# A 31-tap depthwise convolution split into even and odd samples, three half-length filters in sixteen 32x32 tiles of TensorE

## The chip, the core and the metric

One Trainium2 (trn2) chip, one core. The time is the device time in microseconds from launch to end of one execution. The kernel is one program for a whole network block of two parts. Times of several executions agree closely, so a median of three is given.

## What is computed

The reference runs a first transformer block (attention in three branches, a linear recurrence, a feed-forward part) and then a second one with two layers. The change is in the second block. Cut to what matters, one layer of it is:

```python
h = h + 0.5 * swiglu_ffn(rms_norm(h), w_gate_up, w_down)        # ffn "a"
q, k, v, ca, cg = split(rms_norm(h) @ w_in)
attn = sliding_window_attention(rope(q), rope(k), v, sinks)     # 8 heads of 64
u = ca * sigmoid(cg)                                            # 256 tokens x 512 channels
y = depthwise_conv(u, conv_w, taps=31, causal) + conv_b
conv = silu(layer_norm(y, ln_g, ln_b))
h = h + concat(rms_norm(attn), rms_norm(conv)) @ w_out
h = h + 0.5 * swiglu_ffn(rms_norm(h), ...)                      # ffn "b"
e = rms_norm(p @ w_ple)                                         # 256 -> 1024, the "embedding"
h = h + sigmoid(h @ w_ple_gate) * e
```

All data are float32. There are 256 tokens, 1024 features, 512 channels in the convolution, and two such layers. Each channel has its own 31 taps, and y at token s is the sum over j of w[j] * u[s - 30 + j].

## The kernel before, in words

The kernel is written engine by engine: SyncE (SP) loads weights, ScalarE (ACT), VectorE (DVE), GpSimd (POOL) and TensorE (PE) each run a list of instructions in a fixed order, and semaphores tie them together. Each engine works its list strictly in order, so the order written there is the schedule. The two layers are unrolled; only the wide chunks of the feed-forward parts run in hardware loops.

**Weights and products.** A matrix product is a "chunk": 512 output columns for 256 tokens. Its weights come in units of two k-tiles (256 x 512; one k-tile for w_ple) through a ring of 8 stage buffers. ACT copies a unit to w_hi in the reduced format fp32r (`split`, L760), DVE subtracts to get w_lo (`split`, L1417), and PE multiplies hi by hi, hi by lo and lo by hi (L2375 to L2377), each product of 512 columns being one instruction. There are 4 hi/lo slots, so ACT can split a unit only when PE has used the unit four before it. Chunks write alternately to the two PSUM buffers `acc[0]` and `acc[1]`. `CHUNKS` counts them, and a chunk waits until the buffer's last user has been read (`acc_free`). PSUM has two more pairs of banks: `turns` (two banks `turn[0]`, `turn[1]`, used in rotation for transposes and small results, counted by `TURNS`, released by `turn_free`) and `pair` (two banks for scores and the convolution; `score` is its first, counted by `SCORES`). That is all of PSUM. A float32 product that isn't split (transposes L2388, scores L2413, the convolution L2863, means L2930, L2942, L2959) is two instructions on PE, each with its own weight load.

**The order of a layer on PE** around the change (L2856 to L2964): chunks Lq, Lkv, Lcg and Lca with the attention's small products between them, then

- `Lple0`, the first half of p @ w_ple (two k-tiles of 6 products), and ahead of its second k-tile the transposes of the first half of u (`conv_in_turn(0)`, L2913);
- the transposes of the second half of u (L2919), then `Lple1`, the second half of p @ w_ple (12 products);
- the convolution (`conv`, L2867), which waits for `s_in_place` (u_t written), `s_diag` and `s_mixo`;
- a wait for `s_mixlo` (x_lo of the attention half), then `Lout_a0` with the row means of the squared attention output ahead of its first k-tile (L2942) and the first mean over the features ahead of its third (`feature_means(0)`, L2926); `Lout_a1` with the second mean ahead of its first k-tile; `Lout_c0` with the row means of the convolution's half ahead of its last k-tile (L2959); `Lout_c1`.

**The convolution before.** The 512 channels lie on partitions in quads of 32. A tap is a diagonal 32x32 matrix. Two neighbouring taps share one product: partitions 0 to 31 of a pair of quads hold u and partitions 32 to 63 hold u shifted by one token, and the weights are two diagonals on top of each other (64 rows, 32 columns). `diag` holds them for 14 pairs of taps, written by DVE during the chunk `La_dn0` (`diagonals`, L2099 to L2110, eight instructions). PE uses eight tiles of 64x32 at once: 4 groups of channels by 2 row groups, each product with 256 columns (all tokens). There are two halves, each of 14 pairs of taps:

```python
for half in range(2):
    wait(pe, s_in_place, Count(half + 1, [(layer, 2)]))
    for j in range(PAIRS_PE):
        mm = conv_round(half, ..., j == 0, j == PAIRS_PE - 1)
```

To bring the shifted copies in place, ACT and DVE each write eight 32x256 pieces per half from the transposes' bank to `u_t` (`shifted_pairs` L587, L1293, L2160). The last three taps are left to DVE, straight from that bank with per-partition weights and the bias (`late_taps`, L2165 to L2182, into y_late), and `y = pair + y_late` (L2200) follows the convolution. The taps themselves reach `taps2` earlier, in chunk d0 of the first block: POOL loads them in two DMAs to `rawt` (L725), PE transposes them, and DVE moves them with 33 small copies (L1994, L1997).

**The layer norm.** DVE adds y by pairs of channel groups into two `group_sums` (`sum_groups`, L2205); PE multiplies each by a matrix of 1/512 into `score`, adding the two (L2930); DVE centres y (L2220); ACT squares it (L1311), DVE sums again (L2205), PE makes the second mean, ACT takes the root (L1321), DVE the reciprocal (L2231) and the scaling (L2234). ACT then applies silu and writes x_hi (L1328, L1334), DVE x_lo (L2238), for the four k-tiles of `Lout_c0` and `Lout_c1`. A third sum of squares gives the row means (L2959).

**ACT's order** in this stretch (L1284 to L1350): split Lple1; split Lout_a0 unit 0; the shifted copies of half 0; split Lout_a0 unit 1; the copies of half 1; the square of the attention output `att_sq` (L1296), whose halves POOL adds (L740, L743); x_hi of the attention half (L1300); both halves of e_ple out of PSUM (`embedding_out`, L1224); split Lout_a1; the squares of e_ple's first half (L1230); a table load and the root of the row means (L1316); the layer norm's part.

**DVE's order** (L2141 to L2262): u (L2147), split Lple1, a copy of the attention's last result (L1577), for each half the shifted copies and the late taps, split Lout_a0, x_lo of the attention half (L2193), split Lout_a1 unit 0, y, the sums, split Lout_a1 unit 1, the reciprocal of the row means' root, the centring, the sums of squares, the residual of Lout_a0 (L1489), and so on.

## Time and profile before

| | |
|---|---|
| median of 3 runs | 1395.59 us (1395.32 to 1395.7) |
| the profiled execution | 1395.72 us, its span 1393.9 us |
| PE busy | 1382.3 us, 99% of the span, 8063 instructions and as many weight loads |
| DVE busy, ACT busy | 973.1 us (70%), 827.2 us (59%) |
| granted TensorE clock | 0.999 of full speed on average |
| DMA | 249.62 MB, mean 179 GB/s |

The profile is one execution. The span runs from the first to the last instruction on the core; the execution's own time is 1.8 us more. Busy PE time counts pipelined instructions to their modelled ends, so neighbours overlap: what an instruction costs PE is the distance from its start to the next start, not its duration. PEld are weight loads, which run beside the products.

### The profile page before, as it was taken

To read this page: it belongs to the slowest core of one execution; us is meant where nothing else is said; L and a number is where in the kernel's file an instruction comes from. 1 tells how busy PE (TensorE), PEld (TensorE's weight loads), DVE (VectorE), ACT (ScalarE), POOL (GpSimd) and SP (SyncE) were. 2 spreads that over 40 slices of the span, in tenths; PEclk is the share of its full clock that TensorE was granted. 3 is DMA by queue.
4 is the path that set the end of the run, shared out by engine and by line. 5 is a ranking of instruction groups with operands and counts; after the bars stand their busy time and mean duration, and the time that the engine had idled before them with its cause. 6 is when DMAs were issued, how large, how long until landed. Compare 5 with 4: busy or idle time off the path is not lost.

```text
span 1393.9 us, 21622 instructions
## 1 busy us (share of the span) xinstructions
PE 1382.3 (99%) x8063; PEld 1163.7 (83%) x8063; DVE 973.1 (70%) x1408; ACT 827.2 (59%) x1267; POOL 21.4 (2%) x33
## 2 busy tenths in 40 slices
PE   9999999999999999999999999999999999999997
PEld 7777788888888888887888888888888878888886
DVE  5878866775657777568876675676775779777755
ACT  7689755554356554478765554565544687655544
POOL 2100000000000000000000000000000000000000
PEclk9999999999999999999999999999999999999999
DMA  9933555566566666443566665566655435666650
GB/s 289 342 95 107 166 194 175 193 194 197 191 183 202 186 188 203 152 152 114 153 197 193 191 213 185 167 188 190 194 197 156 149 106 152 205 187 189 214 186 31
DMA packets 130157, 249.62 MB, mean 179 GB/s; under 512 B 8552, under 2 KB 12992, under 8 KB 130080
## 3 DMA queue, kind: packets, MB, share of 16 engines
q1 hardware_dynamic: 127680, 240.58, 54.8%
q0 software_dynamic: 2240, 7.73, 1.8%
q8 instruction: 50, 0.82, 0.2%
q10 hardware_dynamic: 160, 0.27, 0.1%
q14 instruction: 27, 0.22, 0.0%
HBM read 247.49 MB, written 1.05 MB: 178 GB/s over the span
## 4 chain that ended last, share of the span: by engine, by line
PE 99%; DVE 0%; ACT 0%; issue 0%; POOL 0%; DVEq 0%; ACTq 0%; POOLq 0%
PE acc L2375 16%; PE acc L2377 16%; PE acc L2376 16%; PE acc L2741 14%; PE pair L2741 7%; PE acc L2747 7%; PE turns L2741 6%; PE pair L2747 4%; PE turns L2747 3%; PE turns L2388 3%; PE pair L2863 2%; PE pair L2413 1%; PE turns L2434 1%; PE acc L2460 1%; PE turns L2529 0%; PE pair L2510 0%
## 5 line engine op out<-in xcount | busy, mean ns | idle before, releaser
L1417 DVE TENSOR_TENSOR w_lo<-stage,w_hi 128x1024 fp32r<-128x1024 f32 (+2 forms) x462 | 549.8, 1200 | 293.5 <-ACT w_hi L760 288.1
L760 ACT ACTIVATE w_hi<-stage 128x1024 fp32r<-128x1024 f32 (+2 forms) x462 | 475.6, 1039 | 405.4 <-PE acc L2377 195.5
L2741 PE MATMUL acc<-x,w_hi 128*128 128x512 f32 x832 | 229.1, 393 | 0.0
L2741 PEld LDWEIGHTS acc<-x,w_hi 128*128 128x128 f32 x832 | 149.3, 189 | 26.1 <-DVE x L1471 0.8
L2375 PE MATMUL acc<-w_hi,x_hi 128*128 128x512 f32 (+2 forms) x432 | 170.5, 395 | 0.1
L2377 PE MATMUL acc<-w_hi,x_lo 128*128 128x512 f32 (+2 forms) x432 | 163.8, 379 | 0.0
L2376 PE MATMUL acc<-w_lo,x_hi 128*128 128x512 f32 (+2 forms) x432 | 163.8, 379 | 0.0
L2375 PE MATMUL acc<-w_hi,g_hi 128*128 128x512 f32 x352 | 137.4, 390 | 0.0
L2376 PE MATMUL acc<-w_lo,g_hi 128*128 128x512 f32 x352 | 137.0, 389 | 0.0
L2377 PE MATMUL acc<-w_hi,g_lo 128*128 128x512 f32 x352 | 137.0, 389 | 0.0
L2747 PE MATMUL acc<-x,w_lo 128*128 128x256 f32 x832 | 136.2, 282 | 0.0
L2747 PEld LDWEIGHTS acc<-x,w_lo 128*128 128x128 f32 x832 | 122.5, 190 | 8.1
L2741 PE MATMUL pair<-x,w_hi 128*128 128x512 f32 x448 | 123.4, 390 | 0.0
L2741 PE MATMUL turns<-x,w_hi 128*128 128x512 f32 x384 | 102.8, 390 | 0.0
L2741 PEld LDWEIGHTS pair<-x,w_hi 128*128 128x128 f32 x448 | 84.1, 188 | 18.2
L2375 PEld LDWEIGHTS acc<-w_hi,x_hi 128*128 128x128 f32 x432 | 81.3, 188 | 20.9 <-issue 6.5
L2377 PEld LDWEIGHTS acc<-w_hi,x_lo 128*128 128x128 f32 x432 | 81.2, 188 | 15.9
L2376 PEld LDWEIGHTS acc<-w_lo,x_hi 128*128 128x128 f32 x432 | 81.4, 188 | 13.3
L2741 PEld LDWEIGHTS turns<-x,w_hi 128*128 128x128 f32 x384 | 72.1, 188 | 15.5
L2377 PEld LDWEIGHTS acc<-w_hi,g_lo 128*128 128x128 f32 x352 | 66.1, 188 | 13.7
L2375 PEld LDWEIGHTS acc<-w_hi,g_hi 128*128 128x128 f32 x352 | 66.1, 188 | 13.5
L2376 PEld LDWEIGHTS acc<-w_lo,g_hi 128*128 128x128 f32 x352 | 66.1, 188 | 13.4
(388 smaller groups left out, 1778.3 us busy)
## 6 DMA issues: line engine op xcount, KB each, us to landing
stage<-in_ffn_w_gate_up SPq DMA_DIRECT2D x176, 512.0 KB, 3.7
stage<-in_ffn_w_down SPq DMA_DIRECT2D x88, 512.0 KB, 4.4
stage<-in_w_ff SPq DMA_DIRECT2D x64, 512.0 KB, 4.1
stage<-in_w_in SPq DMA_DIRECT2D x62, 512.0 KB, 4.4
stage<-in_w_out SPq DMA_DIRECT2D x16, 512.0 KB, 3.8
stage<-in_w_ple_gate SPq DMA_DIRECT2D x16, 512.0 KB, 4.3
stage<-in_w_lru_up SPq DMA_DIRECT2D x8, 512.0 KB, 3.7
stage<-in_w_o SPq DMA_DIRECT2D x8, 512.0 KB, 4.4
```

The source lines that it names most:

```text
L760: act.activation(w_hi[:, n.slot(SPLIT), 0:t, 0:w], stage[:, n.slot(STAGE), 0:t, 0:w], ACT.Copy).then_inc(hi_done, 1)
L1417: dve.tensor_tensor(w_lo[:, n.slot(SPLIT), 0:t, 0:w], stage[:, n.slot(STAGE), 0:t, 0:w], w_hi[:, n.slot(SPLIT), 0:t, 0:w].bitcast(F32), AL ...
L2375: pe.matmul(dst, xh, wh, start=kt == 0, stop=False)
L2376: pe.matmul(dst, xh, wl, start=False, stop=False)
L2377: mm = pe.matmul(dst, xl, wh, start=False, stop=kt == last)
L2388: mm = pe.transpose(turn[n.slot(2)][0:cols_in, at:at + rows_in], src, ident[0:rows_in, 0:rows_in])
L2413: mm = pe.matmul(pair[:, i, k * w:(k + 1) * w], q[half, 2 * g + a, t * P:(t + 1) * P], keys[half, kbase + g, 0:w], start=k == 0, stop=k == ...
L2434: mm = pe.matmul(turn[n.slot(2)][i * HD:(i + 1) * HD, at:at + 2 * P], v(0 if m == 0 else x, g), src, start=m == 0 or x == 0, stop=m == 0 o ...
L2460: return pe.matmul(acc[c][:, t, :], rows[:, i * UNIT_K + q, t * P:(t + 1) * P], weights[:, n.slot(SPLIT), q, :], start=start, stop=stop)
L2741: pe.matmul(banks[m], w_hi[:, n.slot(SPLIT), q, m * P:(m + 1) * P], x2[:, kt, :], start=kt == 0, stop=False)
L2747: mm = pe.matmul(banks[m][:, S:], w_lo[:, n.slot(SPLIT), q, m * P:(m + 1) * P], x2[:, kt, 0:S], start=False, stop=kt == KD - 1)
L2863: mm = pe.matmul(pair[c * QUAD:(c + 1) * QUAD, k, half * S:(half + 1) * S], weights(rows_in, n), src(rows_in, n), start=first, stop=last)
```

## The change

The convolution is computed on even and odd samples ("phases"). With e and o the even and odd samples of u, and with the 32 taps (the 32nd is zero) also split in two interleaved sets of 16, each phase of the output needs two 16-tap filters of 128 samples, four in all. Three do: one filter on the odd samples with the difference of the sets, one on the even samples with another difference, and one on the sum e + o, whose result enters both phases. `taps2` now holds the three sets, `u_t` the two phases, `u_sum` their sum.

- Each filter is 16 taps x 16 tiles of 32 rows by 32 columns with 128 columns moving. The first and the third filter write to `pair` and `turns` (one bank for each row group), the sum's filter to both `acc` buffers, for which `CHUNKS` has two more entries and `TURNS` two more (`Lconv`).
- All 31 taps are done by PE; the late taps and the shifted copies are gone. ACT copies one bank of transposed u to `u_t` and DVE the other, each in one instruction; DVE writes `u_sum` in one. ACT moves the sum's result with the bias to `conv_sum` in four instructions, and y is `pair` or `turns` plus `conv_sum`.
- DVE writes twelve groups of 16 diagonals (512 elements) in place of eight of 14 (448). The first four wait for the last g_lo of the feed-forward part, since they lie in its buffers.
- u is written in two instructions with its blocks of 32 channels permuted.
- Both transposes of u stand ahead of the second k-tile of `Lple0`. `Lple1` stands behind the convolution, and so does, on ACT, the second half of e_ple, between the two splits of `Lout_a1`.
- Each mean over the features is one product of `all_sums`, for which DVE adds the two `group_sums` first; the row means likewise. `feature_means(0)` stands ahead of the first k-tile of `Lout_a0`, not the third, and the wait for `s_mixlo` there too.
- The taps are loaded by eight small DMAs behind a memset and moved by five DVE instructions.

```diff
-TAP_PAIRS = (TAPS2 + 1) // 2
-PAIRS_PE = 14
-LATE = TAPS2 - 2 * PAIRS_PE
+PHASES = 2
+TAPS_P = (TAPS2 + 1) // PHASES
+S_P = S // PHASES
+FILTERS = 3
...
+        def conv_bank(r):
+            return (pair, turns)[r // 2][:, r % 2, :]
+        def sum_bank(r, layer):
+            return acc[CHUNKS.at(f"Lu_sum{r // 2}", 0, layer).slot(2)][:, r % 2, 0:S_P]
+        def in_phases(half):
+            return u_t[:, :, 2 * half:2 * half + 2, TAPS_P - 1:].rearrange("p h a n -> p a h n")
+        def of_tokens(x):
+            return x.rearrange("p (a n h) -> p a h n", a=2, h=PHASES)
...
@@ ACT
                 split("Lple1", layer)
+                act.wait_ge(s_zero, 3)
+                n = TURNS.at("Lu", 0, layer)
+                wait(act, turn_done, n + 1)
+                act.activation(in_phases(0), of_tokens(turn[n.slot(2)][:, :]), ACT.Copy).then_inc(turn_free[n.slot(2)], 1)
                 split("Lout_a0", layer, units=[0])
-                act.wait_ge(s_zero, 3)
-                for k in range(2):
-                    if k == 1:
-                        split("Lout_a0", layer, units=[1])
-                    n = TURNS.at("Lu", k, layer)
-                    wait(act, turn_done, n + 1)
-                    for copy_to, copy_from in shifted_pairs(k, range(KC // 2), turn[n.slot(2)]):
-                        ins = act.activation(copy_to, copy_from, ACT.Copy)
-                    ins.then_inc(s_shifted, 1)
+                embedding_out(0)
                 wait(act, s_mixo, Count(2, [(layer, 1)]))
...
-                for c in range(2):
-                    embedding_out(c)
-                split("Lout_a1", layer)
+                split("Lout_a0", layer, units=[1])
                 embedding_squares(0)
+                wait(act, s_conv_sum, Count(1, [(layer, 1)]))
+                for r in range(KC):
+                    at = V2["conv_b"] + r
+                    ins = act.activation(conv_sum[:, r, :], sum_bank(r, layer), ACT.Identity,
+                                         bias=vec2[:, layer, at:at + 1])
+                    if r % 2:
+                        ins.then_inc(acc_free[CHUNKS.at(f"Lu_sum{r // 2}", 0, layer).slot(2)], 1)
+                split("Lout_a1", layer, units=[0])
+                embedding_out(1)
+                split("Lout_a1", layer, units=[1])
...
@@ DVE
-                for half in range(2):
-                    shifted_half(half)
-                    late_taps(half)
+                n = TURNS.at("Lu", 1, layer)
+                wait(dve, turn_done, n + 1)
+                dve.tensor_copy(in_phases(1), of_tokens(turn[n.slot(2)][:, :])).then_inc(turn_free[n.slot(2)], 1)
+                turns_read(dve, "Lu", 2, layer)
+                dve.tensor_tensor(u_sum, u_t[:, 0, :, :], u_t[:, 1, :, :], ALU.add).then_inc(s_u_sum, 1)
                 split("Lout_a0", layer)
...
-                split("Lout_a1", layer, units=range(1))
-                wait(dve, s_conv, Count(1, [(layer, 1)]))
+                wait(dve, turn_done, TURNS.at("Lconv", 1, layer) + 1)
                 for k in range(2):
+                    evacuated(dve, f"Lu_sum{k}", layer)
                     of = slice(2 * k, 2 * k + 2)
...
                 wait(dve, s_yin, Count(2, [(layer, 2)]))
-                for half in range(2):
-                    sum_groups(y, half)
-                split("Lout_a1", layer, units=range(1, 2))
+                for k in range(2):
+                    dve.sem_inc(turn_free[k], 1)
+                summed = note(dve.tensor_tensor(group_sums[:, :, :], y[:, 0:2, :], y[:, 2:4, :], ALU.add))
+                sum_halves(summed)
+                split("Lout_a1", layer)
...
                 for half in range(2):
                     wait(dve, s_ysq, Count(half + 1, [(layer, 4)]))
-                    sum_groups(ysq, half)
+                    summed = sum_groups(ysq, half)
+                sum_halves(summed)
...
@@ PE
+                def conv_taps(src, weights, bank):
+                    for q in range(TAPS_P):
+                        for n in range(KC):
+                            for r in range(KC):
+                                rows_in = slice(r * QUAD, (r + 1) * QUAD)
+                                mm = pe.matmul(bank(r)[n * QUAD:(n + 1) * QUAD, :], weights[rows_in, n, q, :],
+                                               src[rows_in, n, q:q + S_P], start=q == 0, stop=q == TAPS_P - 1)
                     return mm
                 def conv():
-                    for half in range(2):
-                        wait(pe, s_in_place, Count(half + 1, [(layer, 2)]))
...
+                    turns_read(pe, "Lu", 2, layer)
+                    conv_taps(u_t[:, 1, :, :], diag[:, :, 1, :, :], lambda r: conv_bank(r)[:, 0:S_P])
+                    wait(pe, s_u_sum, Count(1, [(layer, 1)]))
+                    for k in range(2):
+                        c = CHUNKS.at(f"Lu_sum{k}", 0, layer)
+                        wait(pe, acc_free[c.slot(2)], c.lap(2))
+                    conv_taps(u_sum, diag_sum, lambda r: sum_bank(r, layer)).then_inc(s_conv_sum, 1)
+                    conv_taps(u_t[:, 0, :, :], diag[:, :, 0, :, :],
+                              lambda r: conv_bank(r)[:, S_P:S]).then_inc(turn_done, 2)
...
-                chunk("Lple0", pl_hi, pl_lo, layer, ready=lambda kt: conv_in_turn(0) if kt == 1 else None)
-                conv_in_turn(1)
-                chunk("Lple1", pl_hi, pl_lo, layer)
-                wait(pe, s_mixo, Count(2, [(layer, 1)]))
+                chunk("Lple0", pl_hi, pl_lo, layer, ready=conv_in_turns)
                 wait(pe, s_diag, Count(1, [(layer, 1)]))
                 free(SCORES, score_free, "Lsum", 0, layer)
                 conv()
+                chunk("Lple1", pl_hi, pl_lo, layer)
...
                     free(SCORES, score_free, "Lsum", i, layer)
-                    for half in range(2):
-                        wait(pe, s_group_sum, Count(2 * i + half + 1, [(layer, 6)]))
-                        mm = pe.matmul(score[:, 0:S], mean, group_sums[:, half, :], start=half == 0, stop=half == 1)
-                    mm.then_inc(score_done, 1)
+                    wait(pe, s_group_sum, Count(i + 1, [(layer, 3)]))
+                    pe.matmul(score[:, 0:S], mean, all_sums, start=True, stop=True).then_inc(score_done, 1)
                 pe.wait_ge(s_zero, 3)
-                wait(pe, s_mixlo, Count(2, [(layer, 2)]))
```

## Rows read from the trace of the kernel before

**Rows 1.** The page: busy us (share) xinstructions, granted clock in 40 slices, instruction queue.
```profile
PE 1382.3 (99%) x8063; PEld 1163.7 (83%) x8063; DVE 973.1 (70%) x1408; ACT 827.2 (59%) x1267; POOL 21.4 (2%) x33
...
PEclk9999999999999999999999999999999999999999
...
q8 instruction: 50, 0.82, 0.2%
```

**Rows 2.** The page: the chain that ended last, by engine.
```profile
PE 99%; DVE 0%; ACT 0%; issue 0%; POOL 0%; DVEq 0%; ACTq 0%; POOLq 0%
```

**Rows 3.** Timeline of PE, first layer: start us, us, engine, line, operation, count.
```profile
648.73 0.39 PE L2377 MATMUL acc<-w_hi,pl_lo 128*128 128x512 f32 x1
649.05 13.17 PE L2863 MATMUL pair<-u_t,diag 64*32 64x256 f32 x448
662.15 0.61 PE L2942 MATMUL turns<-masks,xs 128*128 128x1 f32 x4
```

**Rows 4.** The same, second layer.
```profile
1139.26 12.32 PE L2863 MATMUL pair<-u_t,diag 64*32 64x256 f32 x448
1152.21 0.58 PE L2942 MATMUL turns<-masks,xs 128*128 128x1 f32 x4 [0.63 <-issue]
```

**Rows 5.** Timeline of DVE, second layer.
```profile
1150.44 1.67 DVE L2193 SCALAR_TENSOR_TENSOR x_lo<-mixt,vec,x_hi 128x256 fp32r<-128x256 f32 x4
...
1153.16 1.28 DVE L2200 TENSOR_TENSOR y<-pair,pt 128x512 f32<-128x512 f32 x2
```

**Rows 6.** Timeline of PEld over 0.09 us: one round's weight loads.
```profile
649.29 0.15 PEld L2863 LDWEIGHTS pair<-u_t,diag 64*32 64x32 f32 x8
```

**Rows 7.** Groups of PEld in the first layer's convolution: count, busy us, mean ns.
```profile
L2863 PEld LDWEIGHTS pair<-u_t,diag 64*32 64x32 f32 x448 | 9.4, 105 | 3.7 <-issue 1.2
```

**Rows 8.** Timeline of PE: 16 fp32 instructions of 128 columns in two tiles.
```profile
613.30 1.16 PE L2413 MATMUL pair<-kt,qt 64*128 64x128 f32 x16
```

**Rows 9.** Timeline of PE: the two means over the features, then the row means.
```profile
665.44 1.02 PE L2930 MATMUL pair<-sig,masks 128*128 128x256 f32 x4
666.12 0.58 PE L2375 MATMUL acc<-w_hi,x_hi 128*128 128x512 f32 x1
...
669.07 1.02 PE L2930 MATMUL pair<-sig,masks 128*128 128x256 f32 x4
...
679.83 0.95 PE L2959 MATMUL pair<-masks,sig 128*128 128x1 f32 x8
```

**Rows 10.** Timeline of PE ahead of the convolution, first layer.
```profile
643.94 0.60 PE L2388 MATMUL turns<-ct,sm 128*128 128x128 f32 x4
645.53 0.39 PE L2377 MATMUL acc<-w_hi,pl_lo 128*128 128x512 f32 x1
```

**Rows 11.** Timeline of DVE ahead of the convolution, first layer.
```profile
643.94 0.42 DVE L1577 COPY mixt<-turns 128x256 f32<-128x256 f32 x1
```

**Rows 12.** Groups of DVE from 532 to 562 us: count, busy, mean ns, idle before.
```profile
L1417 DVE TENSOR_TENSOR w_lo<-stage,w_hi 128x1024 fp32r<-128x1024 f32 x12 | 14.6, 1222 | 7.8 <-ACT w_hi L760 7.6
L2105 DVE TENSOR_TENSOR diag<-vec,taps 128x448 f32<-128x448 f32 x8 | 4.4, 617 | 0.0
```

**Rows 13.** Timeline of ACT around the layer norm, first layer.
```profile
652.42 1.06 ACT L1296 ACTIVATE xs<-mixt 128x1024 f32<-128x1024 f32 x1
653.38 1.69 ACT L1300 ACTIVATE x_hi<-mixt,vec 128x256 fp32r<-128x256 f32 x4
655.10 1.94 ACT L1224 ACTIVATE e_ple<-acc 128x1024 f32<-128x1024 f32 x2
...
660.16 1.28 ACT L1316 ACT_TABLE_LOAD   x1
```

**Rows 14.** Timeline of DVE around the layer norm, first layer.
```profile
666.51 1.29 DVE L2220 SCALAR_TENSOR_TENSOR y<-pair,y 128x512 f32<-128x512 f32 x2 [0.28 <-PE pair L2930]
667.94 0.98 DVE L2205 TENSOR_TENSOR sig<-sm 128x256 f32<-128x256 f32 x2
669.36 1.41 DVE L1489 SCALAR_TENSOR_TENSOR h<-acc,stat,h 128x512 f32<-128x512 f32 x2 [0.43 <-PE acc L2377]
```

More of the change, by code:

```diff
@@ L723, in _ @@
             wait(pool, s_rstd, RSTD.at("norm2", 1))
+            pool.memset(rawt, 0.0).then_inc(s_raw_rows, 1)
+            pool.wait_ge(s_raw_rows, 1)
             for l in range(LAYERS):
-                pool.dma_start(rawt[:, l, :], a["conv_w_2"][l].rearrange("j (r p) -> (j r) p", p=P)).then_inc(s_raw, 16)
+                by_tile = a["conv_w_2"][l].rearrange("j (r a m) -> a j r m", a=KC, m=QUAD)
+                for tile in range(KC):
+                    pool.dma_start(rawt[tile * QUAD:tile * QUAD + TAPS2, l, :].rearrange("j (r m) -> j r m", m=QUAD),
+                                   by_tile[tile]).then_inc(s_raw, 16)
             wait(pool, s_h, RESIDUAL.at("d", 3))
@@ L1229, in embedding_squares @@
                 for t in range(TT):
-                    act.activation(hid2[:, t, :, :].rearrange("p t n -> p (t n)"), e_ple[:, t, c * COLS:(c + 1) * COLS],
+                    if c or t:
+                        wait(act, s_ple, Count(2 * c + t, [(layer, 4)]))
+                    act.activation(pt2[:, 1, 0:COLS], e_ple[:, t, c * COLS:(c + 1) * COLS],
                                    ACT.Square, scale=1.0 / D ** 0.5,
@@ L2954, in row_means @@
                     if kt == 3:
-                        wait(pe, s_group_sum, Count(6, [(layer, 6)]))
+                        wait(pe, s_group_sum, Count(3, [(layer, 3)]))
                         free(SCORES, score_free, "Lsum", 2, layer)
                         for t in range(TT):
-                            for half in range(2):
-                                mm = pe.matmul(score[:, t:t + 1], group_sums[:, half, t * P:(t + 1) * P], mean[:, 0:1],
-                                               start=half == 0, stop=half == 1)
+                            mm = pe.matmul(score[:, t:t + 1], all_sums[:, t * P:(t + 1) * P], mean[:, 0:1],
+                                           start=True, stop=True)
                         mm.then_inc(score_done, 1)
```

147 lines of the change are left out of this document (63 added, 84 removed).

## The prediction

> **What bounds the kernel now.** I read the page first: TensorE is busy 99% of the span, at the full granted clock in all 40 slices [rows 1], and the chain that ended last is 99% PE [rows 2]. So a microsecond counts only if PE itself gets or loses it, by its own instructions or by a wait; DVE (70%) and ACT (59%) matter where PE stands waiting for them. Next comes the timeline of PE around the convolution. In the first layer 448 fp32 instructions of 256 columns run from 649.05 us until the row means start at 662.15: 13.10 us [rows 3]. In the second they run from 1139.26 to 1152.21, 12.95 us, of which 0.63 us is a gap before the row means [rows 4]; DVE's timeline names it: the last x_lo of the attention half ends at 1150.44 + 1.67 = 1152.11 [rows 5]. One instruction lasts 0.375 us to its end, so 448 in 12.32 us are 56 rounds of eight tiles with a period of (12.32 - 0.375) / 55 = 0.217 us [rows 4]. That is the time in which 256 columns pass twice. The eight weight loads of a round leave within 0.15 us, the last of them lasting 0.105, so they are (0.15 - 0.105) / 7 = 6.4 ns apart [rows 6, 7]. Within a round PE issues for 45 ns and then streams.
>
> **The convolution.** The three filters have 16 taps each over 128 columns, in sixteen tiles: 3 x 16 = 48 products per tile, each two instructions, so 96 rounds of sixteen (1536 instructions and as many loads). No row shows sixteen tiles. The nearest rows give a period from two sides. Half of 0.217 is 0.109 us, and sixteen starts 6.4 ns apart need 0.103: they just fit. The score products, fp32 of 128 columns in two tiles, take (1.16 - 0.285) / 7 = 0.125 us a round where the last lasts about 0.285, but with weights of 128 columns [rows 8]. I take 0.112, near the lower end, because its tiles have the same 32-column weights, and keep 0.107 and 0.125. That gives 96 x 0.112 = 10.75 us and 0.2 for the drain behind it, 10.95 in place of 13.10 and 12.95: **-2.15 and -2.0 us** (with 0.125: -0.9 and -0.75). The second layer's gap is counted here: it goes because the second embedding product now stands between the convolution and the row means.
>
> On the supply of instructions the trace proves only the rate of now, 896 records in 12.3 us or 13.7 ns each; asked for are 3072 in 10.75, or 3.5 ns each. The 50 packets of the instruction queue take 0.2% of 16 engines' span, 0.2% x 16 x 1394 / 50 = 0.9 us apiece, and hold 16.4 KB [rows 1]. The Trainium skill ("Runtime: NRT & Kernel Launch", Instruction fetch mechanics) says that such a block is 256 instructions and that PE's memory holds 2048 of them. By it 3072 records are twelve blocks, 10.8 us if they come one behind the other with nothing ahead, and eight of them are there already. The trace agrees with the block: 50 packets can't carry 16,126 records unless the bodies of the loops stay resident.
>
> A rule of the skill speaks against the change: "TensorE: Matmul & The Clock Gate", Wait — 56ns, not 53.3ns, gives about 25 ns as the least distance of two matmul starts. By that rule the convolution would take 1536 x 0.025 = 38 us. The loads of rows 6 are 6.4 ns apart, but for eight only; sustained, rows 4 have 26.7 ns a product, so the trace doesn't exclude it.
>
> **The means.** Each mean over the features is two fp32 products of 256 columns (four instructions, (1.02 - 0.378) / 3 = 0.214 us apart by their own group [rows 9]) and becomes one: 2 x 0.214 saved, twice a layer, 0.86. The row means go from eight instructions to four, at (0.95 - 0.24) / 7 = 0.10: 0.41 saved [rows 9]. **-1.27 us a layer**, all on PE's queue.
>
> **Ahead of the convolution.** Both turns of u now stand behind the first k-tile of the first embedding product; the 2.9 us of the second no longer cover the copies. The first turn starts at 643.94 [rows 10]; the second needs the bank that DVE's copy leaves at 644.36 [rows 11], so it runs about 644.4 to 645.1 with its latency. Then ACT and DVE each copy one bank of 512 elements, 0.64 us by half of the 1.28 of two such reads [rows 5]: in place at 645.8. PE meanwhile has six products, up to about 646.3 (in rows 10 the same six end 0.23 us behind 645.53, 1.8 us after the turn started). **No wait**, slack 0.5 us. DVE gives up 32 shifted copies and the late taps (both engines had 3.1 to 3.5 us per half) for one copy and one sum of 572 elements. u, now two instructions with permuted blocks, costs DVE perhaps 0.1 more and has 1 us of cover.
>
> **Diagonals.** Eight instructions of 448 elements (4.4 us) become twelve of 512, 4.4 x 12/8 x 512/448 = 7.5 us. DVE idles 7.8 us in that stretch [rows 12]; 3.1 more fits. Zero; with no cover it would be up to 3.1 us a layer. The taps' 33 small copies become five; POOL issues eight small DMAs instead of two and a memset, over 100 us before they are read. Zero.
>
> **ACT in the convolution.** Behind its copy: a split (1.06), one half of e_ple (1.94 / 2), the square (1.06), x_hi (1.69) [rows 13], a split, the squares of the embedding (about 1.7), the four moves of the sums (about 1.3): 8.8 us, within 10.95. The first half of e_ple frees the bank of the second filter, which PE wants 3.6 us after the start; ACT is there after some 2.2.
>
> **Behind the convolution.** Let E be its end. PE: twelve products, 2.95 us by the distance of 666.12 and 669.07 [rows 9], then the row means 0.5, so mean 0 is wanted at E + 3.5. DVE: y 1.28, one sum of 512 elements 0.65, one of 256 0.42, with gaps 2.6: in time. Mean 1 is wanted at E + 3.5 + 0.43 + 5.7 = 9.6. ACT is what is **late next**: the second half of e_ple can start only at E + 2.95 (0.97), then a split 1.06, the table load 1.28 [rows 13], the root 0.26: E + 6.5. DVE waits for that before it centres (1.29), while ACT splits and then squares twice 0.62: E + 9.1; the last sums, now with one more step of 0.42 behind two of 0.38 [rows 14], end at about E + 10.0. **+0.4 us of wait a layer** (between 0 and 1.5). The chain from mean 1 to the first product of the convolution's half of w_out starts with the residual (1.41) [rows 14] as before and stays. The row means of the convolution's half had about 1.1 us of slack and lose 0.4.
>
> **The sum.** -2.15 - 2.0 - 2 x 1.27 + 2 x 0.4 = -5.9 us. The profiled execution took 1395.72 (span 1393.9 with 1.8 around it), so 1389.8; the median of the runs, 1395.59, is 0.13 below it: **1389.7**. A measurement of this kernel can tell about 0.2%, 2.8 us.
>
> **Rivals.**
> (1) Sixteen tiles don't run at once: the array or the four row groups that add into the same partitions let eight through, and a round takes 0.217 us. Then the convolution takes 96 x 0.217 + 0.2 = 21.0 us, +7.9 and +8.1; with the means the time is about 1409: slower. For it: no row has more than eight. Against it: the change gives each row group its own bank, and the starts are 6.4 ns apart. It decides from a period of (13.0 + 1.27 - 0.4) / 96 = 0.144 us. Instructions fetched late would cost the same way, but as gaps: the 50 packets served at most 16,126 / 50 = 322 records each [rows 1], so 3072 take ten or more; at 0.9 us they just fit, at twice that, one by one, they are 18 us and the time is near 1403. Together 0.15.
> (2) The issue floor of the skill's page binds. As a mechanism here it is one product each 25 ns, just under the 26.7 of rows 4: 25.4 us more a layer, near 1444. 0.04.
> (3) The convolution runs as forecast or near 0.125, but ACT's late second half costs PE 1 to 2 us a layer or the slack ahead of the convolution is negative: 1392 to 1394. For it: five things stand on ACT's queue before the root. 0.18.
> My forecast, -4.8 to -7.7 us, has 0.61; 0.02 is left for what I don't see.
>
> **Numbers.** Faster by over 2.8 us: the forecast and half of (3), 0.70. Within: the rest of (3) and a little of (1), 0.12. Slower: 0.18. The range goes down to 1387 (a period of 0.107, no waits: -7.7, and a little) and up to 1396, which takes in all of (3); what is left out is (1) and (2). The likeliest case's own range is 1387.5 to 1391.
>
> **What would show it.** In the changed timeline 1536 instructions in 10.6 to 10.9 us from first start to last end; no gap before them; the first instruction of the second embedding product 0.2 to 0.3 us behind the last start; means of two instructions; a gap of 0.2 to 0.6 before mean 1 with DVE's last sum as its releaser. A convolution over 13.9 us, or gaps in it, would prove me wrong on the sign; a wait over 1 us at the first filter, at mean 0 or at mean 1 would be rival 3.

## The result, and the profile after

The changed kernel takes 1459.24 us (median of six runs, 1455.67 to 1462.26) beside 1395.64 us for the kernel before (1395.32 to 1395.96): a ratio of 1.0455, 95% interval [1.0444, 1.0466], **slower by 63.6 us**. I had forecast 1389.7. The profiled execution took 1459.78 us with a span of 1458.0.

Page of the changed kernel, the lines that answer to [rows 1, 2]:

```profile
PE 1415.1 (97%) x10223; PEld 1189.3 (82%) x10223; DVE 956.5 (66%) x1342; ACT 818.5 (56%) x1245; POOL 31.4 (2%) x40
...
PE   9999999999999999996999999999999969999997
...
PEclk9999999999999999996999999999999988999999
...
q8 instruction: 67, 1.10, 0.3%
...
PE 93%; issue 2%; DVE 2%; ACT 2%; DMA 1%; POOL 0%; DVEq 0%; ACTq 0%; POOLq 0%
```

Two slices of the span have a dent, one per layer, in PE's busy share and near it in the granted clock; before, all forty were full. "issue" is now in the chain: time in which PE waited for nothing that the profile shows. And the instruction queue has 67 packets in place of 50.

The stretches come next: the convolution of each layer, from its first product to the instruction behind it. Columns: the stretch, its length, then busy time (count) of PE, PEld, DVE, ACT, POOL, then granted clock, DMA share, GB/s.

```profile
646.52:689.16 42.64, 27.33 (x1537) 21.44 (x1536) 4.29 (x7) 6.98 (x15) 2.66 (x3) 0.78 0.17 50
1168.46:1211.76 43.30, 28.44 (x1538) 22.06 (x1537) 4.27 (x7) 6.98 (x15) 1.98 (x2) 0.74 0.14 43
```

42.6 and 43.3 us stand where 13.10 and 12.95 stood [rows 3, 4]: +59.9 of the 63.6 us. PE is busy for 27 to 28 of these 43 us, and no other engine is what it waits for: DVE works 4.3 us in there and ACT 7.0. The timeline of PE in the first layer (start, duration, idle time before) shows the empty parts as gaps:

```profile
650.57 0.30 PE L2878 MATMUL pair<-u_t,diag 32*32 32x128 f32 x2 [1.24 <-issue]
654.58 0.30 PE L2878 MATMUL pair<-u_t,diag 32*32 32x128 f32 x2 [2.10 <-issue]
658.32 0.30 PE L2878 MATMUL pair<-u_t,diag 32*32 32x128 f32 x2 [1.83 <-issue]
```

These three are 4.0 and 3.7 us apart, and over both layers neighbouring ones are 3.3 to 4.0 us apart. The starts of all 1536 products of layer 1 have eleven such gaps, behind product 199, 327, 455 and so on (counted from 0), **each 128 products**, with 19.0 us in sum from start to start; layer 2 has eleven behind 182, 310, ... with 18.7. A product is two records of PE's program, its weight load and its matmul, so 128 products are 256 records. What moves by DMA meanwhile is the other half of the reading. The DMA view of the changed kernel from 646 to 690 us (40 slices of 1.1 us):

```profile
GB/s 371 374 52 203 229 78 194 168 298 15 0 0 15 0 0 15 0 0 15 0 0 15 0 0 0 15 0 0 15 0 0 0 15 0 0 15 0 0 15 0
...
q8 instruction: 12, 0.20, 1.9%
```

From 656 us on nothing moves but one block of 0.20 MB / 12 = 16.4 KB every third or fourth slice. These are PE's instructions: twelve blocks for 3072 records. The queue is otherwise empty, so no other traffic holds them up. By the packets' own times one lasts 0.9 to 1.4 us, PE goes on 1.3 to 1.6 us behind its end, and one comes each 3.3 to 4.0 us.

What lay within my forecast is there too: no wait ahead of the convolution, means of two instructions, and the wait of 0.54 us at mean 1, where I had said 0.4, with DVE's last sum as its releaser:

```profile
694.27 0.50 PE L2962 MATMUL turns<-masks,xs 128*128 128x1 f32 x4
694.63 0.68 PE L2951 MATMUL pair<-sig,masks 128*128 128x256 f32 x2
...
701.33 0.67 PE L2951 MATMUL pair<-sig,masks 128*128 128x256 f32 x2 [0.54 <-DVE sig L2217]
```

One more wait of 0.31 us a layer is new, at 713.85 and 1236.25, for a split of DVE (w_lo); I had forecast none there.

### The profile page after: what moved, and what is told of

Read it like the earlier page. It is cut to its first block, busy times and chain, and to the rows that moved or that the text cites. A ratio compares the mean times of both kernels' runs of the same rounds, so it can differ in the third digit from the quotient of the medians.

```text
span 1458.0 us, 25868 instructions
## 1 busy us (share of the span) xinstructions
PE 1415.1 (97%) x10223; PEld 1189.3 (82%) x10223; DVE 956.5 (66%) x1342; ACT 818.5 (56%) x1245; POOL 31.4 (2%) x40
## 4 chain that ended last, share of the span: by engine, by line
PE 93%; issue 2%; DVE 2%; ACT 2%; DMA 1%; POOL 0%; DVEq 0%; ACTq 0%; POOLq 0%
PE acc L2390 14%; PE acc L2391 14%; PE acc L2392 14%; PE acc L2756 13%; PE pair L2756 7%; PE acc L2762 7%; PE turns L2756 6%; PE pair L2762 4%; PE turns L2762 3%; PE turns L2403 3%; PE turns L2878 1%; PE pair L2878 1%; PE acc L2878 1%; DMA stage<-in_w_in 1%; PE pair L2428 1%
## 5 line engine op out<-in xcount | busy, mean ns | idle before, releaser
L2756 PEld LDWEIGHTS pair<-x,w_hi 128*128 128x128 f32 x448 | 84.2, 188 | 18.2
```

The lines of the kernel that those rows point to most:

```text
L2756: pe.matmul(banks[m], w_hi[:, n.slot(SPLIT), q, m * P:(m + 1) * P], x2[:, kt, :], start=kt == 0, stop=False)
```

## The experiments

**Theory A**, taken from those lines: PE's instructions arrive 256 at a time, one block per 3.7 us once what was read ahead is used up, and the convolution asks for 3072 of them in a row. **Rivals** from the prediction: the sixteen tiles contend for the array, or each product has a floor of about 25 ns (1536 x 25 = 38.4 us, which is uncomfortably near to what was measured). One product, as I count it, is one PE instruction, and each fp32 matmul of the code gives two. Two of the texts below are miscounted: in the loop kernel five sixths of the records need not be fetched, not four fifths (512 are left of 3072), and the kernel of four taps has 384 products and 768 records a layer.

### Twice the columns: 256 instead of 128

```
                                 mm = pe.matmul(bank(r)[n * QUAD:(n + 1) * QUAD, :], weights[rows_in, n, q, :],
-                                               src[rows_in, n, q:q + S_P], start=q == 0, ...
+                                               src[rows_in, n, q:q + S_P].unsqueeze(1).to_broadcast([QUAD, 2, S_P]), ...
```

(the three banks are 256 columns wide)

> The changed kernel with 256 moving columns in each convolution product instead of 128 (the same 1536 products a layer, the same 3072 records, twice the columns; the convolution's values are not the reference's). Theory A, PE's instruction supply gives one block of 256 records each 3.7 us: nothing changes, convolution 41 to 44 us a layer, whole kernel 1450 to 1465 us, a gap still behind each 128 products. Rival, the sixteen tiles contend for the array (42.6 us is streaming): twice the columns, 80 to 86 us a layer, kernel about 1540. Rival, a floor of about 25 ns per product (1536 x 25 = 38.4 us): unchanged as in A, but without gaps behind each 128.

One execution: 1457.43 us. The stretches:

```profile
648.48:691.58 43.10, 33.07 (x1538) 22.30 (x1537) 4.28 (x7) 6.99 (x15) 2.69 (x3) 1.00 0.17 50
1168.68:1211.43 42.75, 33.45 (x1537) 22.40 (x1536) 4.27 (x7) 7.00 (x15) 2.01 (x2) 1.00 0.13 43
```

Twice the streaming costs nothing, 43.1 and 42.75 us. In the starts of the products the gaps are again 128 apart (behind 199, 327, 455, ...), only shorter (14.1 us in sum), since the streaming of 256 columns fills part of them. So it is not the array. The clock stayed at 1.00 here, against 0.78 and 0.74: the fall of the clock is not what makes 43 us either.

### Eight of the sixteen tiles

```
                         for n in range(KC):
-                            for r in range(KC):
+                            for r in (n % 2, 2 + n % 2):
```

> The changed kernel with 8 of the 16 tiles of each tap (768 products a layer; half of the convolution is left out). Theory A: about 190 products run from what is already fetched (2 us), the other 578 at 128 per 3.7 us (16.7 us): 18 to 19.5 us a layer, gaps behind each 128, kernel 1405 to 1413. Rival, sixteen tiles in flight contend and eight do not: rounds of eight at 0.112 us, 10.9 us a layer, kernel about 1392. Floor of 25 ns: 19.2 us, evenly spaced, no gaps.

1410.3 us (one execution), half of the convolution left out.

```profile
646.77:667.26 20.49, 12.23 (x770) 10.73 (x769) 4.28 (x7) 6.99 (x15) 2.66 (x3) 1.00 0.30 97
1144.38:1164.35 19.97, 13.60 (x770) 11.86 (x769) 4.27 (x7) 6.98 (x15) 1.99 (x2) 0.91 0.28 87
```

20.5 and 20.0 us, 0.5 to 1 us over theory A's range and nearly twice the 10.9 of "eight tiles stream freely". The gaps are behind product 199, 326, 454, 582 and 710, up to 2.26 us. Even spacing, as the floor of 25 ns wants it, is not what the trace shows.

### The same products from a loop

```
-                    conv_taps(u_t[:, 1, :, :], diag[:, :, 1, :, :], lambda r: conv_bank(r)[:, 0:S_P])
+                    odd_bank = lambda r: conv_bank(r)[:, 0:S_P]
+                    with pe.Fori(0, 11) as j:
+                        conv_taps(u_t[:, 1, :, :], diag[:, :, 1, :, :], odd_bank, range(4))
+                    conv_taps(u_t[:, 1, :, :], diag[:, :, 1, :, :], odd_bank, range(2))
...
-                    conv_taps(u_sum, diag_sum, ...)
+                    conv_taps(u_sum, diag_sum, ..., range(1))
```

(the last filter has one tap as well; the first filter's products are repeated in place of what the other two leave out)

> The changed kernel with as many convolution products (1536 a layer, 16 tiles, 128 columns) but from a hardware loop: a body of 4 taps (128 products, 256 records) run 11 times, and 4 more taps straight. The second and third filter have one tap each, so the values are not the reference's; what PE executes is the same number of the same products with four fifths fewer records to fetch. Theory A: no gap of over 1 us behind each 128 products; 7 to 12.5 ns per product, 11 to 19 us, with 11 branches of some tenths of a microsecond: 13 to 24 us a layer, granted clock 0.9 or more, kernel 1395 to 1420. Both rivals (tiles contend, floor of 25 ns per product) leave it at 38 to 43 us a layer, kernel 1450 or more. If a body of 256 records is fetched anew each time round, A too gives 40 us.

1414.74 us (one execution), 44.5 below the changed kernel with the same 1536 products.

```profile
646.52:669.10 22.58, 22.29 (x1537) 18.45 (x1536) 4.27 (x7) 6.52 (x14) 2.66 (x3) 1.00 0.27 85
1146.18:1168.78 22.60, 22.29 (x1537) 18.46 (x1536) 4.27 (x7) 6.52 (x14) 2.00 (x2) 1.00 0.23 72
```

22.6 us, clock 1.00, and not one distance of over 0.28 us between two starts. PE is busy but for 0.30 us behind the last product, where it waits for ACT. The DMA view has two instruction packets in this stretch, which are its 512 records. This is the run that decides: same products, same tiles, same columns, and the gaps go when the records need not be fetched. Theory A holds, and both rivals in their form of 38 to 43 us are out.

It also says that **theory A is not all**. Without any gap the convolution still takes 22.6 us, 14.3 ns per product; I had forecast 0.112 us for sixteen, 7 ns each. With this loop in place of the convolution the change would still lose 19 us.

### A body of 512 records

```
-                    with pe.Fori(0, 11) as j:
-                        conv_taps(..., range(4))
-                    conv_taps(..., range(2))
+                    with pe.Fori(0, 5) as j:
+                        conv_taps(..., range(8))
+                    conv_taps(..., range(6))
```

> The loop kernel with a body twice as long: 8 taps, 256 products, 512 records, run 5 times (40 of 48 taps), and the rest straight. If PE keeps the 512 records: about 22 to 24 us a layer. If it keeps no more than the one to two blocks of 256 that it had read ahead in the straight code, each time round is fetched anew: gaps behind each 128 products as in the changed kernel, 3.7 us per 128, 38 to 42 us a layer.

1419.52 us (one execution).

```profile
646.49:671.37 24.88, 21.64 (x1538) 18.95 (x1537) 4.29 (x7) 6.52 (x14) 2.66 (x3) 1.00 0.25 78
...
650.96 0.26 PE L2878 MATMUL turns<-u_t,diag 32*32 32x128 f32 x1 [1.68 <-issue]
```

One gap stands behind product 198, in the first pass of the body, and one in the straight part at the end; the four passes behind the first, 1024 products, have none of that size. So 512 records stay. The DMA view counts 4 instruction packets in the whole stretch, as against 12: 512 records of the body and 512 behind it. Products, tiles and banks are the same in the first pass as in the later ones, so what costs is records that are new.

This run also tells what a turn costs. A later pass takes 3.53 us for 256 products, and one of the kernel above 1.86 us for 128. The difference is 13.0 ns a product, and 0.19 us are left for each pass. The straight code agrees: between two gaps at full clock the changed kernel starts 128 products within 1.63 us, 12.8 ns each.

### Columns, weights, tiles and their order in the loop

Four of these kernels are the loop of 128 products a turn with one thing changed: 64 moving columns; 256; weights of 16 columns; and the loops over r and n exchanged. The fifth takes 64 columns in eight tiles, with twice the turns of half the body.

> The loop kernel (1536 products a layer, body of 128, 128 columns: 22.0 us) with 64 moving columns per product. Theory B, each product with its weight load takes PE at least about 14 ns whatever its columns: 21 to 22 us again. Rival, the loop's 22.0 us is streaming of tiles that share the array: 11 to 12 us.

> The loop kernel with 256 moving columns per product. Streaming alone with sixteen tiles at once: 0.213 us of product over 16 tiles, 13.3 ns each, as much as the least distance of theory B (14.3), so 22 to 27 us a layer. Rival, tiles share the array so that only about eight stream at once: 26.7 ns per product, 41 us. Straight code with 256 columns took 42.8 us with gaps behind each 128 products; theory A says that in the loop they are gone.

> The loop kernel (128 moving columns) with weights of 32 rows by 16 columns in place of 32 by 32, so that each product writes half of its tile's partitions. The loop runs so far took 11.9, 14.3 and 19.6 ns per product at 64, 128 and 256 moving columns: a part of about 9 to 10 ns that does not depend on them. If that part is the weight load's columns (32 per product): 9.5 to 10.5 ns per product, 15 to 16 us a layer. If it is a fixed cost of an instruction pair: 14.3 ns, 22 us.

> The loop kernel (128 columns, sixteen tiles, 14.3 ns per product, 22.0 us a layer) with the loops over tiles exchanged: four tiles of one row group behind one another, each in another column group, instead of four of one column group. If the order of groups sets the 14.3 ns it changes: towards 7 to 10 ns, 11 to 16 us, or above 20 ns. If it is a cost of each product, 22 us again.

> The loop kernel with 64 moving columns in eight of the sixteen tiles, and twice the taps, so 1536 products again (body of 64 products, 23 turns). Sixteen tiles with 64 columns took 11.9 ns a product with the loop's turns and 10.0 without. A fixed part per product: the same 10 ns, 15.4 us a layer and 23 turns of up to 0.28 us, 16 to 22 us. If only the columns in flight count, half the tiles give twice the time per product: 20 ns, 30 us or more.

The first layer's stretch of each, 64 columns:

```profile
646.78:665.69 18.91, 17.69 (x1537) 15.48 (x1536) 4.29 (x7) 6.52 (x14) 2.67 (x3) 1.00 0.32 103
```

256 columns:

```profile
646.69:677.33 30.64, 30.56 (x1538) 23.37 (x1537) 4.27 (x7) 6.52 (x14) 2.67 (x3) 1.00 0.21 63
```

weights of 16 columns:

```profile
646.54:668.63 22.09, 21.78 (x1537) 17.06 (x1536) 4.29 (x7) 6.52 (x14) 2.67 (x3) 1.00 0.28 87
```

tiles in the other order:

```profile
646.98:669.60 22.62, 22.30 (x1538) 18.49 (x1537) 4.28 (x7) 6.53 (x14) 2.67 (x3) 1.00 0.27 86
```

eight tiles of 64 columns:

```profile
648.41:670.82 22.41, 20.42 (x1538) 16.61 (x1537) 4.27 (x7) 6.53 (x14) 2.66 (x3) 1.00 0.27 85
```

From the first to the last of the 1536 starts, divided by 1535:

| loop kernel | us a layer | ns per product | a pass, us (products) | without 0.19 us a pass, ns (estimate) | whole kernel, us (one execution) |
|---|---|---|---|---|---|
| 64 columns, 16 tiles | 18.30 | 11.9 | 1.54 (128) | 10.5 | 1407.48 |
| 64 columns, 8 tiles | 21.61 | 14.1 | 0.917 (64) | 11.4 | 1416.54 |
| 128 columns, 16 tiles | 22.02 | 14.3 | 1.86 (128) | 13.0 | 1414.74 |
| the same, order exchanged | 22.05 | 14.4 | 1.86 (128) | 13.0 | 1415.17 |
| the same, weights 16 columns wide | 21.52 | 14.0 | 1.82 (128) | 12.7 | 1413.74 |
| 256 columns, 16 tiles | 30.19 | 19.7 | 2.52 (128) | 18.2 | 1430.91 |

The 0.19 us are measured at 128 columns. That they hold at the other widths is an estimate; for it speaks that the last pass, which has no turn behind it, is 0.10 to 0.14 us shorter than the others in every row.

My expectation of a constant 14 ns fell with the first row, and so did its rival, streaming alone, which wanted 11 to 12 us. What holds is in between: at 64 columns eight tiles take 11.4 ns a product and sixteen 10.5, where columns in flight would have given double. At 128 columns half the weight's columns and another order change 2% or nothing. So down to 64 columns a product costs 10 to 11 ns that more tiles do not divide. Longer ones cost more on top, though less than the streaming of eight tiles would (19.7 ns at 256 columns, where the eight tiles of the kernel before take 26.7). Whether fewer columns would go below 10 ns was not run. For 256 columns I had expected 22 to 27 us, and it took 30.2. How the two add up inside PE, the runs don't say.

How could a rate of 6.4 ns be read before the change [rows 6]? Windows over the starts, changed kernel: the first 0.24 us of the convolution, the 2.0 us behind, and the same for the first block behind a gap.

```profile
646.52:646.76 0.24, 0.24 (x33) 0.24 (x33) 0.24 (x1) 0.14 (x1) 0.00 (x0) 1.00 1.04 376
646.76:648.76 2.00, 2.00 (x174) 1.87 (x145) 1.24 (x2) 2.00 (x3) 0.08 (x1) 1.00 0.74 282
650.57:650.81 0.24, 0.24 (x31) 0.24 (x33) 0.00 (x0) 0.24 (x1) 0.24 (x2) 1.00 1.01 393
650.81:652.21 1.40, 1.40 (x128) 1.29 (x96) 1.05 (x1) 1.37 (x4) 0.61 (x1) 1.00 0.42 107
```

33 products start within 0.24 us, 7 ns each, and then the rate falls to 2.0/174 = 11.5 ns (products still in flight at a window's start are counted too, so if anything it is slower). The same happens behind a gap. My reading, which no run tests, is that some thirty products lie ready when PE has stood still, and go out fast. The eight loads of a round in the kernel before would then never come to the end of that store: PE streamed for 0.17 us, and it filled again.

### Four taps of sixteen

```
-                    for q in range(TAPS_P):
+                    for q in range(4):
```

> The changed kernel with 4 of 16 taps of each filter (192 products, 384 records a layer; the convolution's values are not the reference's). Theory A: all of it lies in what is fetched ahead or nearly so: 1.3 to 2.7 us without a long gap, clock kept, the embedding products behind it 2.9 us instead of 5.1. Then the rest of the change alone speaks: 1395.6 - 2 x 10.9 - 2 x 0.9 = 1372 us; up to 1382 where with the convolution so short the splits, the diagonals or a load become what PE waits for. The floor of 25 ns: 4.8 us a layer, 1377. Tiles contending: 5.3 us a layer.

1388.56 us, ratio 0.9957 [0.9943, 0.9971]. The kernel leaves out three quarters of the convolution. Its 768 records a layer are three blocks, so the times of the text above rest on a wrong count. By theory A with the right count that is 190 products in 2 us and (384 - 190) / 128 x 3.7 = 5.6, together 7.6 us.

```profile
646.20:654.74 8.54, 5.72 (x385) 4.79 (x385) 4.28 (x7) 6.88 (x15) 2.66 (x3) 1.00 0.66 198
1131.87:1140.66 8.79, 5.79 (x385) 4.79 (x384) 4.27 (x7) 6.88 (x15) 1.98 (x2) 1.00 0.60 187
```

8.5 and 8.8 us, with two gaps in each layer. In this execution (1386.63 us) the convolution is 4.56 + 4.16 = 8.7 us shorter than before and the kernel 9.1. The five runs of this kernel lie between 1386.6 and 1391.8 us, 7.2 us below before by their median, so it can't tell what the rest of the change brings. The next one can.

### The rest of the change, at a convolution of equal length

```
-                    with pe.Fori(0, 11) as j:
+                    with pe.Fori(0, 6) as j:
```

> The changed kernel with its convolution cut to 896 products a layer, run from a loop (six times 128, and 128 straight), so that at the loop's measured 14.3 ns per product it lasts about 12.9 us, as long as the convolution before (13.1, 12.9). What is left over against before is the rest of the change: order of the embedding product, one copy per half, means, diagonals, u_sum, four conv_sum copies. My sum for the rest was -0.9 us a layer, 1393.5 us in all; from the runs so far (loop, eight tiles, four taps) it comes to between +0.3 and +1 us a layer, 1396 to 1397.5.

1396.29 us, ratio 1.0006 [0.9997, 1.0015]. The kernel leaves out 640 of the 1536 products a layer.

```profile
646.18:659.45 13.27, 12.97 (x897) 10.83 (x897) 4.27 (x7) 6.52 (x14) 2.68 (x3) 1.00 0.49 145
```

The stretch is 13.27 us in both layers, 0.5 us in sum over before, and the kernel 0.7 us over it. So all else in the change, the order, the copies, the diagonals and the means, costs **0.2 us, nothing that can be told from zero** (the interval is +-1.3 us; the profiled execution alone, 1395.74 us, would give -0.5). I had it at -1.75.

### The means alone

```
-                    for half in range(2):
-                        wait(pe, s_group_sum, Count(2 * i + half + 1, [(layer, 6)]))
-                        mm = pe.matmul(score[:, 0:S], mean, group_sums[:, half, :], start=half == 0, stop=half == 1)
+                    wait(pe, s_group_sum, Count(i + 1, [(layer, 3)]))
+                    pe.matmul(score[:, 0:S], mean, all_sums, start=True, stop=True).then_inc(score_done, 1)
```

(the kernel before, with the row means and DVE's sums changed alike)

> The kernel before with one part of the change alone: one product over all_sums per mean (8 products and 4 row products fewer a layer, one DVE addition more per mean). Every theory of the convolution leaves this part alone, so it shows what that part of my sum (1.27 us a layer) is worth. Expected 1393.1 us, 2.5 us below before; if the additions only move the wait (each mean now hangs on two DVE additions in a row), 1395 to 1396.

1395.89 us, ratio 1.0005 [0.9996, 1.0014]: the 2.5 us are not there. The timeline of PE in the first layer says where they went:

```profile
665.29 0.39 PE L2385 MATMUL acc<-w_hi,x_lo 128*128 128x512 f32 x1
665.78 0.67 PE L2937 MATMUL pair<-sig,masks 128*128 128x256 f32 x2
666.10 0.59 PE L2383 MATMUL acc<-w_hi,x_hi 128*128 128x512 f32 x1
...
669.76 0.67 PE L2937 MATMUL pair<-sig,masks 128*128 128x256 f32 x2 [0.54 <-DVE sig L2212]
670.08 0.58 PE L2383 MATMUL acc<-w_hi,x_hi 128*128 128x512 f32 x1
...
682.29 0.47 PE L2383 MATMUL acc<-w_hi,x_hi 128*128 128x512 f32 x1 [0.30 <-DVE w_lo L1418]
```

From mean to next product it is 0.32 us instead of 0.68 [rows 9], as I had it. But mean 0 comes 0.49 us behind the product ahead of it (0.22 before), mean 1 waits 0.54 us for the second of two additions in a row, and DVE, which has one addition more each time, is 0.30 us late with a split (w_lo) for which PE did not wait before. Three savings of 0.36, 0.36 and 0.4 us, and three waits of 0.27, 0.54 and 0.30.

### x_lo between the two splits

```
-                split("Lout_a0", layer)
+                split("Lout_a0", layer, units=[0])
                 for k in range(2):
                     wait(dve, s_mixhi, Count(k + 1, [(layer, 2)]))
...
+                split("Lout_a0", layer, units=[1])
```

> As the run with one product per mean, and on DVE the attention half's x_lo between the two splits of Lout_a0 instead of behind both, so that PE's 0.63 us wait behind layer 2's convolution goes. Expected 1392.5 us, 3.1 us below before. If the second split of Lout_a0 is then what PE waits for, as much as without it (1393.1) or above.

1395.90 us, ratio 1.0003 [0.9994, 1.0012]. The 0.63 us gap ahead of layer 2's row means went, and 0.80 us came back twelve products later, at mean 0:

```profile
1151.68 0.61 PE L2949 MATMUL turns<-masks,xs 128*128 128x1 f32 x4
1155.94 0.67 PE L2938 MATMUL pair<-sig,masks 128*128 128x256 f32 x2 [0.80 <-DVE sig L2213]
```

### Mean 1 one tile later

```
-                chunk("Lout_a1", x_hi, x_lo, layer, ready=lambda kt: feature_means(1) if kt == 0 else None)
+                chunk("Lout_a1", x_hi, x_lo, layer, ready=lambda kt: feature_means(1) if kt == 1 else None)
```

> The kernel before with one product per mean, and mean 1's product ahead of Lout_a1's second tile instead of its first, so that DVE's two additions lie behind three embedding-size products and not behind an idle PE. Run with the mean ahead of the first tile, PE waited 0.54 us there in each layer and the three savings of about 0.35 us were all given back. If nothing downstream of mean 1 is late: 1394.5 us, 1.1 below before. If the centring chain behind it (squares, row means, Lout_c0's rows) has no room: 1395.5 to 1396.

1396.68 us, ratio 1.0009 [1.0000, 1.0018]. The wait at mean 1 is gone, and one of 1.13 us is new, ahead of the convolution's half of w_out:

```profile
672.08 0.59 PE L2937 MATMUL pair<-sig,masks 128*128 128x256 f32 x2
677.93 0.47 PE L2383 MATMUL acc<-w_hi,x_hi 128*128 128x512 f32 x1 [1.13 <-DVE x_lo L2245]
```

So far as these three runs show, the chain from the end of the convolution over y, mean 0, the squares and mean 1 to x_lo is as long as PE's own work beside it, and PE's saving there only uncovers the chain. None of the three versions with the new means is faster than the kernel before.

## Why the prediction was wrong

**The sum of the loss.** Changed kernel 1459.24; without fetches 1414.74 (-44.5); with the convolution at its old length 1396.29 (-18.4); before 1395.6 (-0.7). So 70% of the loss is the supply of instructions (with up to 4 us of a lower clock that came with it, below) and 29% the price of a product. The price alone makes the change slower, as the loop shows. That the supply alone would do so too follows from its rate, twelve blocks of 3.7 us against a convolution of 13.

**The step on the supply of instructions failed first**, in its sentence "at 0.9 us they just fit". I had the right size of a block and the right count, twelve, and took the duration of a packet for the distance of two. The measured distance is 3.3 to 4.0 us while the queue is otherwise empty. The kernel before held the number, and I didn't look at it. Its 896 records in 13.1 us are 3.7 us per 256: in its first layer it ran at the limit. The starts there have two distances of 0.34 and 0.43 us, behind product 314 and 442, 128 apart, and both end 1.3 to 1.4 us behind an instruction packet, as the gaps of the changed kernel do; its second layer has none. They make 0.63 of the 0.85 us between [rows 3] (13.17 us) and [rows 4] (12.32) for the same work, a difference that I had before me and passed over. The rest is a distance of 0.23 us behind product 445, whose cause I don't know.

I gave late fetches, with "tiles don't run at once", 0.15, and priced them at 18 us for a layer's convolution, a kernel of 1403 us; it was 42.6 us a layer and 1459. There the size was off: twice 0.9 us a block instead of 3.7. (Rival 1's own sum comes to 1410 us, not 1409.) The page of the Trainium skill that I cited, "Runtime: NRT & Kernel Launch" (Instruction fetch mechanics), has the block of 256 right, by the twelve packets for 3072 records. Its figure of 2048 instructions that PE's memory holds, which I used for "eight of them are there already", is not borne out as read-ahead: the first gap comes behind product 199 and 182, some 370 to 400 records in.

**The step on the period of a round failed second.** "I take 0.112 near the lower end" came from half of 0.217 us of streaming and eight loads 6.4 ns apart [rows 6]. The loop shows 16 x 14.3 = 229 ns (208 without its turns). That is the number of rival 1, but not its reason: with 256 columns sixteen tiles take 16 x 19.7 = 315 ns a round and not 2 x 229 = 458, and with 64 columns eight tiles are not twice as slow per product as sixteen, but 8% slower. A burst was taken for a rate. The point from which rival 1 decides, 0.144 us a round, held the saving of the means; with all else worth nothing it is 13.0 / 96 = 0.135. Both were passed, for another reason than rival 1's.

**The rule of 25 ns** from the Trainium skill ("TensorE: Matmul & The Clock Gate", Wait — 56ns, not 53.3ns) pointed the right way: a product has a least price. Its number doesn't hold for products in different small tiles: 14.3 ns at 128 columns, 11.9 at 64, turns included. That 38.4 us came so near to 42.6 is chance; the loop tells them apart.

**The means, -1.27 us a layer, were right as a saving and wrong as a gain.** The waits that the additions bring, 0.27 at mean 0 and 0.30 at the split, were missing; I had 0.4 for mean 1 (0.54 measured) and nothing for the others. "DVE ... in time" for mean 0 had left out that PE gets there sooner too.

**The clock.** I had it at full speed. The 0.78 of the first layer is a mean of its two levels, 2.4 GHz up to 670.1 us and 1.2 GHz from there:

```profile
646.52:670.10 23.58, 13.35 (x919) 11.16 (x924) 4.29 (x7) 5.84 (x11) 2.66 (x3) 1.00 0.28 87
670.10:689.16 19.06, 13.97 (x635) 10.28 (x624) 0.00 (x0) 1.14 (x4) 0.00 (x0) 0.50 0.02 5
```

PE had been busy for 13.4 of 23.6 us when it fell. A block of 128 products then took 2.4 us instead of 1.6, but the next one still came 3.5 to 4.0 us behind it, so inside the convolution the low clock cost next to nothing. The products of the second embedding product behind it ran with it:

```profile
689.16:694.27 5.11, 5.11 (x18) 4.00 (x14) 3.40 (x5) 1.06 (x1) 0.00 (x0) 0.52 0.00 2
```

This stretch is at 1.2 GHz but for its last 0.3 us, and it lasts 5.1 us (layer 2: 4.9) where twelve such products take 2.95 at 2.4 GHz [rows 9]. That explains up to 4 us of the 63.6; the run with 256 columns kept its clock and was 1.8 us below the changed kernel's median, in one execution.

**What held**: no wait ahead of the convolution, nothing from the diagonals, no gap behind the second layer's convolution, ACT's list within the cover (busy for 6.5 of 13.3 us where the convolution had its old length), the place of the wait at mean 1 and nearly its size. The steps around the convolution came to 0.2 us where I had -1.75; the two rates inside it decided.

## What to carry to other kernels

Count the records of a straight stretch, not only its array time: here a block of 256 came each 3.7 us, so straight code can't go on below 14.4 ns a record for more than some 400 records, about 29 ns for a load and its product. Put short products in a loop's body (512 records stayed), or make them fewer and longer; the kernel before, with half the tiles and twice the columns, had found just this balance. And where a product is split over more tiles, ask for its own price (10 to 11 ns at 64 columns here, 13 at 128), which more tiles did not divide; a burst of some thirty products doesn't show it.

A saving on PE beside a chain that is as long as PE's own work is worth nothing: look for the chain's slack first.

## What was not expected of the hardware

- 256 PE instructions per 3.3 to 4.0 us with an idle DMA queue, though one fetch of 16.4 KB lasts 0.9 to 1.4 us: they come one at a time, with over 2 us between them.
- Loop bodies of 256 and 512 records run without a fetch behind their first pass; a pass costs 0.19 us beside its products (at 128 columns, from bodies of two lengths).
- 33 products in 0.24 us from a standing start, then 11 to 14 ns each. Of the 14.3 ns of the loop 1.3 are its turns; what makes up the 10 to 11 ns of a product at 64 columns stays open.
- With gaps of 1.1 to 2.4 us in every 3.7 at 128 columns the clock fell to 1.2 GHz after PE had been busy for 13.4 of 23.6 us. With 256 columns, where it was busy for 33 of 43 us, it stayed at 2.4 GHz.
